# The first feed-forward's gate and up projections as seven block products in place of eight

## The reference, cut to what matters

```
xn = rms_norm(x, ffn_norm_g)
gate, up = split(xn @ w_gate_up)          # w_gate_up: 1024 x 5632
x = x + (silu(gate) * up) @ w_down        # w_down: 2816 x 1024
...
def rmsnorm(x, g):
    return x * rsqrt(mean(x * x) + EPS) * g
```

## Time and profile before

| | us |
|---|---|
| median of 3 runs | 3125.1 (3124.98 to 3130.51) |
| profiled execution | 3127.51 |
| its span, first to last instruction | 3125.7 |
| PE busy | 2919.3 (93%) |
| DVE busy | 1598.9 (51%) |
| ACT busy | 1273.6 (41%) |
| POOL busy | 297.0 (10%) |
| mean granted TensorE clock | 0.966 of full speed |

### The profile page before, as it was taken

How to read it: one execution, slowest core, us unless ns; L and a number is a source line. 1 busy time by engine, 2 the same in 40 slices (tenths; PEclk the granted TensorE clock), 3 DMA queues, 4 the chain that set the end, 5 groups by cost and what they waited for, 6 DMA issues and landing times.

```text
span 3125.7 us, 34780 instructions
## 1 busy us (share of the span) xinstructions
PE 2919.3 (93%) x14266; PEld 2321.7 (74%) x14266; DVE 1598.9 (51%) x2284; ACT 1273.6 (41%) x1821; POOL 297.0 (10%) x265
## 2 busy tenths in 40 slices
PE   5999989999999999899999899999999669999994
PEld 4777767777788788788888566666787458888883
DVE  3344533364431234654232455554345579999994
ACT  5344433222121223311111566665213347777774
POOL 1011201000000000222000111111000200000000
PEclk8999989999999999899999899999999789999997
DMA  3110122344511212231211111113334559999994
GB/s 128 55 41 28 41 95 81 95 126 148 145 42 54 98 51 87 54 101 41 68 62 47 41 41 41 41 35 132 105 108 156 210 220 388 392 398 397 398 386 143
DMA packets 232788, 415.69 MB, mean 133 GB/s; under 512 B 26493, under 2 KB 133125, under 8 KB 232117
## 3 DMA queue, kind: packets, MB, share of 16 engines
q1 hardware_dynamic: 213808, 348.16, 31.6%
q0 software_dynamic: 18672, 65.27, 6.2%
q10 hardware_dynamic: 148, 0.04, 0.0%
HBM read 371.38 MB, written 42.05 MB: 132 GB/s over the span
## 4 chain that ended last, share of the span: by engine, by line
PE 89%; DVE 5%; ACT 3%; issue 1%; DMA 1%; POOL 0%; ACTq 0%; DVEq 0%; SPq 0%; POOLq 0%
PE PS L124 84%; PE PS L127 5%; ACT m L130 3%; DVE m L133 2%; DVE m L139 1%; ACT L130 0%; DMA xa_scratch<-m,small 0%; DVE m L175 0%; DVE m L178 0%; DVE m L172 0%; DVE m L142 0%; DMA m<-xa_scratch 0%; DMA m<-in_w_proj_conv_dram 0%; DMA m<-xh_scratch,small 0%; DVE m L136 0%
## 5 line engine op out<-in xcount | busy, mean ns | idle before, releaser
L124 PE MATMUL PS<-m,m 128*128 128x512 f32 (+5 forms) x12498 | 2725.9, 391 | 62.0 <-DVE m L133 32.5
L124 PEld LDWEIGHTS PS<-m,m 128*128 128x128 f32 (+2 forms) x12498 | 2116.6, 185 | 598.0 <-issue 113.8
L133 DVE TENSOR_TENSOR m<-m,m 128x2048 fp32r<-128x2048 f32 (+5 forms) x420 | 704.3, 1698 | 387.5 <-ACT m L130 359.3
L130 ACT ACTIVATE m<-m 128x2048 fp32r<-128x2048 f32 (+3 forms) x438 | 600.6, 1383 | 671.9 <-PE PS L124 361.6
L130 ACT ACTIVATE m<-PS 128x512 f32<-128x512 f32 (+4 forms) x491 | 274.7, 577 | 778.6 <-PE PS L124 594.7
L133 DVE TENSOR_TENSOR m<-PS,m 128x512 f32<-128x512 f32 (+1 forms) x304 | 200.3, 687 | 553.9 <-PE PS L124 495.1
L127 PE MATMUL PS<-ident,m 128*128 128x128 f32 (+2 forms) x1544 | 225.0, 286 | 102.8 <-DVE m L148 36.0
L127 PEld LDWEIGHTS PS<-ident,m 128*128 128x128 f32 (+2 forms) x1544 | 193.8, 148 | 141.4 <-DVE m L148 36.2
L130 ACT ACTIVATE m<-m,small 128x640 f32<-128x640 f32 (+5 forms) x202 | 160.5, 795 | 206.9 <-DVE small L136 141.4
L142 DVE CUSTOM_DVE_ANT_0 m<-PS,m 128x640 f32<-128x640 f32 (+4 forms) x192 | 146.5, 775 | 127.2 <-PE PS L124 118.9
L148 DVE COPY m<-PS 128x512 f32<-128x512 f32 (+1 forms) x176 | 107.0, 617 | 143.6 <-PE PS L127 102.9
(11 more groups left out here) (75 smaller groups left out, 398.2 us busy)
## 6 DMA issues: line engine op xcount, KB each, us to landing
m<-in_w_exp_gate_dram SPq DMA_DIRECT2D x64, 1024.0 KB, 8.6
m<-in_w_exp_up_dram SPq DMA_DIRECT2D x64, 1024.0 KB, 8.7
m<-in_w_exp_down_dram SPq DMA_DIRECT2D x64, 1024.0 KB, 8.1
m<-in_w_mod_dram SPq DMA_DIRECT2D x24, 1024.0 KB, 5.3
m<-in_w_gate_up_dram SPq DMA_DIRECT2D x44, 512.0 KB, 6.7
m<-in_w_in_dram SPq DMA_DIRECT2D x41, 512.0 KB, 3.9
m<-in_w_in_dram SPq DMA_DIRECT2D x12, 1024.0 KB, 5.0
m<-in_w_down_dram SPq DMA_DIRECT2D x10, 1024.0 KB, 5.1
```

Of the source, the lines that this page charges most:

```text
L124: return Unsent() if self.e is None else self.e.matmul(o, l, r, start=first, stop=last, **k)
L130: return Unsent() if self.e is None else self.e.activation(o, i, fn, **k)
L133: return Unsent() if self.e is None else self.e.tensor_tensor(o, a, b, op)
```

## The change: what it does

It multiplies the weights of a step, a 2x2 of blocks (gate/up x two halves of K, A11, A21 for gate's lower and upper K and A12, A22 for up's), with the tokens, a 2x2 of blocks (two halves of K x two halves of the tokens), by Strassen's scheme in Winograd's form: seven products P1 to P7, each of 12 matmuls of 512 columns (4 k blocks x 3), in place of eight. It needs sums of blocks on both sides.

- **Tokens.** x1 is scaled in place by `xt1_scale`, now on DVE alone and with ffn_norm_g as a row (`ffn_row`), so it waits for the stores of x1. Seven operands of 512x512 are transposed and split, four `turn4` each, 28 in all (16 before): three blocks of x1 and T1 to T4, whose differences are made by DVE (T1) and POOL (T2, T3, T4).
- **Weights.** Four sums S1 to S4 of a step are made by POOL (`gu_sums`, 128x512 each). Seven operands of 128x512 are split by ACT and DVE (`gu_high`, `gu_low`) into a ring of eight slots.
- **Results.** P2 adds into P1's bank after ACT has copied P1 (`gu_first`), and P3 into P5's bank after DVE has made C22 from it. DVE makes five combinations a step (`gu_u2`, `gu_u3`, `gu_c22`, `gu_c21`, `gu_c12`), ACT two Silu's, POOL the two gated products (`gu_gated`), and stores them to `h_scratch` in DRAM.
- **Modulation.** It goes in 48 quarters of two k blocks (the same 128 instructions), two quarters in each of steps 1 to 8 and four in each of steps 9 to 16.
- **Down.** SP loads the gated rows back (`h_load`), the first two after `rows_st`; split of pair 0 and of the first down weights lies inside step 21. The second column half goes through K in another order.

The diff, cut to its core (a line of "..." marks what is left out):

```diff
+                pool.dma_start(x1_dram[tile128(i), :], x1[:, i, :]).then_inc(*pool.landed(f"x1_st{i // 4}"))
 
         cc = sm(2, 8)
...
+        def mod_add(dve, q):
+            c = q // 4
+            acc = accs[c % 2]
             dve.wait_ge(f"mod_raw{q % 2}", q)
-            for k in range(4):
+            for k in range(2):
                 for j in mod_rows(c):
-                    s_ = cc[:, j, 4 * half + k:4 * half + k + 1]
-                    if half + k == 0:
+                    s_ = cc[:, j, 2 * (q % 4) + k:2 * (q % 4) + k + 1]
+                    if q % 4 + k == 0:
                         dve.wait_ge("act_in", "silu_c")
                         if c >= 2 and j in mod_rows(c - 2):
                             dve.wait_ge(f"mod_st{c % 2}{j}", c - 2)
...
+        S_of = {S: ar(144 + 2 * n, 4, 128) for n, S in enumerate(("S1", "S2", "S3", "S4"))}
+        ho = [ar(112, 1024), ar(116, 1024)]
+        u2, u3 = ar(124, 512), ar(126, 512)
...
+        def xt1_scale(dve, i):
+
+            dve.wait_ge("rstd", "x1", i // 4)
+            dve.wait_ge("x_again")
+            dve.wait_ge(f"x1_st{i // 4}")
+            dve.scalar_tensor_tensor(x1[:, i, :], x1[:, i, :], rs8[:, i:i + 1], ffn_row, ALU.mult, ALU.mult).then_inc(
+                *dve.did("xt1_scaled", i))
+
+        def xn_diff_dve(dve, i):
+            dve.wait_ge("xt1_scaled", i + 4)
+            dve.wait_ge("xn2_turned", "B11", i)
+            dve.tensor_tensor(x1[:, i, 0:512], x1[:, i + 4, 0:512], x1[:, i, 0:512], ALU.subtract).then_inc(*dve.did("xt1_diff_v", i))
+
+        def xn_diff_pool(pool, T, i):
+            a, b = half512(0), half512(1)
+            pool.wait_ge("xt1_diff_v", i)
+            if T == "T3":
+                pool.tensor_tensor(x1[:, i + 4, a], x1[:, i + 4, b], x1[:, i + 4, a], ALU.subtract).then_inc(*pool.did("xt1_diff_p", T, i))
+            elif T == "T2":
+                pool.tensor_tensor(t2[i], x1[:, i + 4, b], x1[:, i, a], ALU.subtract).then_inc(*pool.did("xt1_diff_p", T, i))
+            else:
+                pool.wait_ge("xt1_diff_p", "T2", i)
+                pool.wait_ge("xn2_turned", "B21", i)
+                pool.tensor_tensor(x1[:, i, b], t2[i], x1[:, i, b], ALU.subtract).then_inc(*pool.did("xt1_diff_p", T, i))
+
+        def turn_xn(pe, T, i):
+            pe.wait_ge(*xn_ready(T, i))
...
+
+        def gu_split(c, P):
+
+            n = (7 * c + GU_ORDER.index(P)) % 8
+            kb = 16 + 16 * ((W_O + n // 4) % 2) + 4 * (n % 4)
+            return tuple(piece(kb + a, 512, F32R).rearrange("p (k n) -> p k n", n=128) for a in (0, 2))
+
+        def gu_high(act, c, P):
+            if c == 22:
+                return
+            m = 7 * c + GU_ORDER.index(P)
+            act.wait_ge(f"w_raw{(W_GU + c) % 2}", W_GU + c)
+            if P in ("P6", "P7", "P5", "P3"):
+                act.wait_ge("gu_sum", c, {"P6": "S2", "P7": "S3", "P5": "S1", "P3": "S4"}[P])
+            if m < 8:
+                act.wait_ge(*w_done.get(W_O + 2 + m // 4, ("w_low", 0)))
+            else:
+                act.wait_ge("gu_acc", (m - 8) // 7, GU_ORDER[(m - 8) % 7])
+            act.activation(gu_split(c, P)[0], gu_source(c, P), ACT.Copy).then_inc(*act.did("w_high", W_GU + c, P))
+
+        def gu_low(dve, c, P):
+            if c == 22:
+                return
+            H, L = gu_split(c, P)
+            dve.wait_ge("w_high", W_GU + c, P)
...
+        def gu_sums(pool, c):
+
+            if c == 22:
+                return
+            v = w_raw(W_GU + c)
+            a11, a12, a21, a22 = (v[:, k:k + 4, n:n + 128] for n in (0, 128) for k in (0, 4))
+            pool.wait_ge(f"w_raw{(W_GU + c) % 2}", W_GU + c)
+            for S, P, a, b, op in (("S1", "P5", a21, a22, ALU.add), ("S2", "P6", S_of["S1"], a11, ALU.subtract),
+                                   ("S3", "P7", a11, a21, ALU.subtract), ("S4", "P3", a12, S_of["S2"], ALU.subtract)):
+                if c:
+                    pool.wait_ge("w_low", W_GU + c - 1, P)
+                if S == "S2":
+                    pool.wait_ge("gu_sum", c, "S1")
+                if S == "S4":
+                    pool.wait_ge("gu_sum", c, "S2")
+                pool.tensor_tensor(S_of[S], a, b, op).then_inc(*pool.did("gu_sum", c, S))
+
+        def gu_product(pe, c, P):
+
+            H, L = gu_split(c, P)
+            Bh, Bl = XN[GU_B[P]]
+            if P == "P2":
+                bank_of["gu_acc", c, P] = bank_of["gu_acc", c, "P1"]
+                pe.wait_ge("gu_silu", c, "s1")
+            elif P == "P3":
+                bank_of["gu_acc", c, P] = bank_of["gu_acc", c, "P5"]
+                pe.wait_ge("gu_up", c, "C22")
+            else:
+                bank_of["gu_acc", c, P] = pe.bank(*{"P1": ("gu_silu", c, 0), "P6": ("gu_up", c, "U2"), "P7": ("gu_up", c, "U3"),
+                                                    "P5": ("gu_up", c, "C12"), "P4": ("gu_up", c, "C21")}[P])
+            pe.wait_ge("w_low", W_GU + c, P)
+            pe.wait_ge("xn2_low", GU_B[P], 3)
+            for k in range(4):
+                t = mm3(pe, ps("gu_acc", c, P), (H[:, k, :], L[:, k, :]), (Bh[:, k, :], Bl[:, k, :]),
+                        k == 0 and P not in ("P2", "P3"), k == 3, **(dict(skip_group_check=True) if P in ("P2", "P3") else {}))
+            t.then_inc(*pe.did("gu_acc", c, P))
+            if c == 21 and P in ("P5", "P3"):
+                w_done[W_GU + 20 + (P == "P3")] = ("gu_acc", c, P)
...
+        def gu_first(act, c):
+            act.wait_ge("gu_acc", c, "P1")
+            if c:
+                act.wait_ge("gu_up", c - 1, "U2")
+            act.activation(gu_s1(c), ps("gu_acc", c, "P1"), ACT.Copy).then_inc(*act.did("gu_silu", c, "s1"))
+
+        def gu_silu0(act, c):
+            act.wait_ge("gu_acc", c, "P2")
+            if c:
+                act.wait_ge("h_out", c - 1, 0)
+            act.activation(sil[0], ps("gu_acc", c, "P2"), ACT.Silu).then_inc(*act.did("gu_silu", c, 0))
+
+        def gu_silu1(act, c):
+            act.wait_ge("gu_up", c, "C12")
+            act.activation(sil[1], sil[1], ACT.Silu).then_inc(*act.did("gu_silu", c, 1))
+
+        def gu_u2(dve, c):
+            dve.wait_ge("gu_silu", c, "s1")
+            dve.wait_ge("gu_acc", c, "P6")
+            dve.tensor_tensor(u2, ps("gu_acc", c, "P6"), gu_s1(c), ALU.add).then_inc(*dve.did("gu_up", c, "U2"))
+
+        def gu_u3(dve, c):
+            dve.wait_ge("gu_up", c, "U2")
+            dve.wait_ge("gu_acc", c, "P7")
+            dve.tensor_tensor(u3, ps("gu_acc", c, "P7"), u2, ALU.add).then_inc(*dve.did("gu_up", c, "U3"))
+
+        def gu_c22(dve, c):
+            dve.wait_ge("gu_up", c, "U3")
+            dve.wait_ge("gu_acc", c, "P5")
+            if c >= 2:
+                dve.wait_ge(f"h_st{c % 2}", c - 2)
+            dve.tensor_tensor(ho[c % 2][:, 512:1024], ps("gu_acc", c, "P5"), u3, ALU.add).then_inc(*dve.did("gu_up", c, "C22"))
+
+        def gu_c21(dve, c):
+            dve.wait_ge("gu_acc", c, "P4")
+            dve.tensor_tensor(ho[c % 2][:, 0:512], u3, ps("gu_acc", c, "P4"), ALU.subtract).then_inc(*dve.did("gu_up", c, "C21"))
+
+        def gu_c12(dve, c):
+            dve.wait_ge("gu_acc", c, "P3")
+            if c:
+                dve.wait_ge("h_out", c - 1, 1)
+            dve.tensor_tensor(sil[1], ps("gu_acc", c, "P3"), u2, ALU.add).then_inc(*dve.did("gu_up", c, "C12"))
+
+        def gu_gated(pool, c):
+            for h in range(2):
+                v = ho[c % 2][:, half512(h)]
+                pool.wait_ge("gu_up", c, "C22" if h else "C21")
+                pool.wait_ge("gu_silu", c, h)
+                pool.tensor_tensor(v, v, sil[h], ALU.mult).then_inc(*pool.did("h_out", c, h))
+            pool.wait_ge("h_out", c, 1)
+            pool.dma_start(h_dram[tile128(c), :], ho[c % 2]).then_inc(*pool.landed(f"h_st{c % 2}", c))
+
+        def mod_at(c):
+
+            if 1 <= c <= 8:
+                return [2 * c - 2, 2 * c - 1]
+            return [16 + 4 * (c - 9) + a for a in range(4)] if 9 <= c <= 16 else []
+
+        def mod_done(c):
+            return [q // 4 for q in mod_at(c) if q % 4 == 3]
+
         x2 = ar(0, 8, 1024)
         hsp = [(rr(32 + 16 * j, 2, 1024), rr(40 + 16 * j, 2, 1024)) for j in range(2)]
...
+
+        def h_tile(m):
+
+            return ar([96, 104, 64, 72, 80, 88, 112, 120, 128, 136, 144][m], 2, 1024)
+
+        def h_load(sp, m):
+            sp.dma_start(h_tile(m), h_dram[256 * m:256 * m + 256, :].rearrange("(a p) n -> p a n", p=128)).then_inc(
+                *sp.landed(f"h_in{m}"))
 
         def ffn_sp(sp):
...
         def ffn_sp(sp):
...
+                for q in mod_at(c):
+                    mod_load(sp, q + 2)
+            sp.wait_ge("rows_st")
+            sp.wait_ge("h_st0", 2)
+            sp.wait_ge("h_st1", 3)
+            h_load(sp, 0)
+            h_load(sp, 1)
+            sp.wait_ge("gu_acc", 21, "P7")
+            sp.wait_ge("h_st0", 10)
+            sp.wait_ge("h_st1", 11)
+            for m in range(2, 6):
+                h_load(sp, m)
```

(165 more changed lines are left out.)

168 lines of the change are left out of this document (45 added, 123 removed), and 4 rows, old and new, of the table SHARED.

## The result

The median is 3098.0 us (3090.5 to 3099.2, 4 runs) against 3125.0 (3123.6 to 3130.5, 4 runs): a ratio of 0.9905 (0.9885 to 0.9925), faster by 0.95%. That is 27 us where 37.6 were forecast: inside the whole range of 3070 to 3110, and 2 us outside the forecast's own range of 3079 to 3096. The profiled execution has a span of 3097.3 us, 28.4 less than before. Where each of these microseconds came from can be read in the trace; the last split of the down projection, at 1274.98 before, is a good mark for the end of all that was changed.

A forecast was written before the change was run, and what follows sets the result against it. PE, busy 93% of the span, was taken to set the time. The terms -57.2 + 12.8 + 7.8 - 1.0 = -37.6 us took 3125.1 to 3087.5, said as 3087; own range 3079 to 3096, whole range 3070 to 3110.

The forecast's parts named there:

- The products: Steps 1 to 21: 84 matmuls for 96, 2.73 us less a step, 57.2 us saved; a step takes 19.1.
- Steps 1 to 8: C22 leaves DVE at 18.0, PE is ready for P3 at 16.4 and stands 1.6 us a step: +12.8 us.
- Steps 9 to 16: Modulation in four places; C22 is out at 15.3, before PE needs it at 16.4: no stall, 0.
- POOL, 0: In the steps, most of POOL's work, at 1.2 us a pass, falls into DVE's idle time: 0 us added.
- The front: Up to step 1: rounds of 4.4 us, P1 from 542.6, P3 waiting for C22; 7.8 us later, bounds 0 and +12.
- The end: Gap before the down projection: 2.7 to 3.8 us for 4.3, so -1.
- Store and reload of h [...] Hidden.: Store has two steps until its buffer is reused; loads of pairs 2 on have 11 us a pair: no cost.
- (a): Rival: no stall in steps 1 to 8, C22 out by 16.4; gain 50.4 us, time 3075; chance 0.15.
- (b): Rival: POOL's sums delay DVE's chain from P2's split to C22 in 16 steps; +20 us, 3107; chance 0.20.
- (c): Rival: the stalls lower PE's clock, 1.8 us a drop, eight of them +14 us: 3101; chance 0.08.
- (d): Rival: exclusion with POOL makes DVE the bound, steps 1 to 16 at 23.5 us; 58 us slower, 3145; chance 0.04.

The follow-up runs named there:

- experiment 3: Changed kernel with the second modulation quarter of steps 1 to 8 placed behind C22 on DVE: 3082.0 us, ratio 0.9850 to the kernel before.
- experiment 4: Changed kernel with P5's next-weight split repeated four times more ahead of C22 in steps 9 to 20: 3118.5 us, ratio 0.9968 to the kernel before.
- experiment 6: Changed kernel with the four weight sums of a step made by DVE ahead of u2, not POOL: 3096.2 us, ratio 0.9895 to the kernel before.
- experiments 1 and 2: Changed kernel, each alone: third down weight group issued before the last five h reloads, 3082.2 us; x1's reload put off until after the fourth down pair, 3082.9 us.
- experiment 5: Changed kernel with POOL's front differences held back until DVE's four are out: 3096.7 us, ratio 0.9894 to the kernel before.

## Why the prediction came out as it did

**The forecast's mechanism was right: a shorter PE, given back in part to DVE's chain before P3.** By its terms:

- **The products, -57.2.** A step without modulation takes 19.12 us for the forecast 19.1 and for 21.80 before, which is 56.4 in 21 steps. Right.
- **Steps 1 to 8, +12.8.** By the trace 11.07 of waits and about 2 of restarts; experiment 3 took 13.3 away. Right in cause. The size is right in part by luck: a wait is 1.38 in the mean for the forecast 1.6, and the restart, which the sum left out, makes up for it. In step 1 (start 571.67) C22 is out at 589.54, 17.9 after the start for the 18.0 worked out. DVE's timeline there:

```profile
584.41 0.68 DVE L134 TENSOR_TENSOR m<-PS,m 128x512 f32<-128x512 f32 x1
585.01 1.28 DVE L134 TENSOR_TENSOR m<-m,m 128x512 fp32r<-128x512 f32 x2
...
586.21 2.73 DVE L140 SCALAR_TENSOR_TENSOR m<-m,small,m 128x512 f32<-128x512 f32 x4
...
588.86 0.68 DVE L134 TENSOR_TENSOR m<-PS,m 128x512 f32<-128x512 f32 x1
```

These are u3, two splits, a quarter of modulation and C22, with no gap between them, each at its forecast price. Ahead of them two misses cancel in this step: P2's split ends 10.7 after the start for 10.1, and the first quarter takes 2.2 for 2.7.

- **Steps 9 to 16, 0.** One wait of 0.33, ended by DVE, where the chain shows the store of a modulation row (8.33 us, at 849.07) ahead, which the next accumulation waits for. The spare was 0.8 for 1.1 (experiment 4).
- **POOL, 0.** Its passes take 1.29 alone and 1.66 to 1.85 beside DVE in the steps, for the 1.2 taken, and they do slow DVE, but in the main in the stretch the prediction named, between C12 and P2's split. The 1.4 us of experiment 6 are what they cost at most. POOL and DVE in step 1:

```profile
578.36 1.75 POOL L134 TENSOR_TENSOR m<-m 128x512 f32<-128x512 f32 x1
...
579.11 1.55 DVE L134 TENSOR_TENSOR m<-m,m 128x512 fp32r<-128x512 f32 x1 [0.15 <-ACT m L131]
```

- **The front, +7.8.** Measured +5.9, 4.6 without what lay ahead of the change. Mis-sized by 3: the rounds took 4.1 us for 4.4, and P1 began at 540.97, not 542.6.
- **The end, -1.0.** As a gap it is -3.2: `h_load` landed sooner (ACT splits h from 996.93, 12.3 into the step for about 14), so DVE is through earlier.
- **"Store and reload of h [...] Hidden."** This is the step that failed. It asked whether the rows of h would come in time for their own pairs, and they do. It did not ask what is late next on the same queue, the weight load behind them on SP, nor what stands behind that load on ACT and DVE, the split of pair 3. Nor did it count the volume, 11 MB of h and 4 MB of x1 within some 49 us (991.9 to 1040.6), at 410 GB/s while the engines are full. The cost is 12.3 us (experiments 1 and 2), seen as +10.9 against before, since the kernel before started its down projection cold after its gap of 4.3 and paid 1.4 there.

With this term, +10.9 as against the kernel before, the forecast of -37.6 becomes -26.7, beside a measured -27 in the median and -28.4 in the span. The other misses nearly cancel, which is luck: steps 1 to 21 gave 42.7 for the forecast 44.4 (1.7 less), the front cost 1.9 less and the gap 2.2 less than forecast. All four together lead from -37.6 to the -29.1 of the table.

**The rivals.** (a) no stall: refuted, the waits are there. (b) POOL in the chain's way: not the cause by experiment 6, 1.4 us at most. (c) the waits lower the clock: refuted for steps 1 to 8, clock 1.00 throughout, though it did happen after 1.88 in experiment 4, after 2.34 in experiment 5 and after 9.39 here. (d) DVE as the bound: refuted, DVE is busy 282 of 432 us. None of the four was the term that was missing.

## What to carry to other kernels

When a kept tensor is sent through DRAM, list what stands behind the reload on its queue and give each of these a due time of its own; a load that waits for the last store holds back every load after it. Do the same for the engine that waits for the load: what is written behind the waiting instruction, here the split of the next pair, is held back with it. Add up the megabytes that are asked for in the same stretch and divide by the rate that the trace shows when the DMA share is 1.0. And an engine at 65% can still be the bound through one chain with a deadline: put work without a deadline (here, the modulation) behind the instruction that frees the bank.
